# A hybrid decoder step on one core: the FFN's seven products in another order, and its two kinds of low parts on swapped engines

## The reference, cut to what matters

```
u = rmsnorm(x, g_ffn) @ w_up              # 1024 -> 4096
x = x + jnp.square(jax.nn.relu(u)) @ w_down   # 4096 -> 1024
y = rmsnorm(x, g_final)
```

## Time and profile before

| | us |
|---|---|
| median of three runs | 1503.9 |
| the profiled execution, its own time | 1504.5 |
| its span, first to last instruction | 1502.7 |
| PE busy in the span | 1412.1 (94%) |
| DVE busy | 1020.5 (68%) |
| POOL busy | 602.2 (40%) |
| ACT busy | 532.2 (35%) |

### The profile page before, as it was taken

One profiled execution on the slowest core, in us unless ns is written; L12 is line 12 of the kernel. 1 busy time (PEld: TensorE's weight loads), 2 busy tenths in 40 slices (PEclk: granted clock), 3 DMA queues, 4 the chain that ended last, 5 costly groups with the idle time before them and its releaser, 6 DMA issues.

```text
span 1502.7 us, 28686 instructions
## 1 busy us (share of the span) xinstructions
PE 1412.1 (94%) x11826; PEld 1242.5 (83%) x11826; DVE 1020.5 (68%) x1759; ACT 532.2 (35%) x917; POOL 602.2 (40%) x454
## 2 busy tenths in 40 slices
PE   6999999999999889898997999999999999999996
PEld 4989989999998566685777979797988989797984
DVE  6883655568852677664527895958687685958588
ACT  6342322322221567543313333332323333332324
POOL 2121221888710000002218572827456372827453
PEclk9999999999999999999999999999999999999998
DMA  7412103722206732297000322131303122131312
GB/s 210 169 42 61 29 15 62 111 67 75 63 8 216 278 120 71 101 384 258 29 3 29 114 67 104 56 114 41 108 23 128 43 87 84 56 115 43 114 32 116
DMA packets 109811, 144.59 MB, mean 96 GB/s; under 512 B 26738, under 2 KB 78774, under 8 KB 107762
## 3 DMA queue, kind: packets, MB, share of 16 engines
q1 hardware_dynamic: 107618, 138.04, 29.3%
q0 software_dynamic: 2064, 4.72, 0.8%
HBM read 126.31 MB, written 21.14 MB: 98 GB/s over the span
## 4 chain that ended last, share of the span: by engine, by line
PE 78%; DVE 11%; issue 6%; ACT 3%; POOL 1%; DMA 1%; SPq 0%; DVEq 0%; ACTq 0%; POOLq 0%
PE PS L343 7%; PE PS L344 7%; PE PS L345 7%; PE PS L2706 6%; PE PS L2708 6%; PE PS L2707 6%; PE PS L2745 5%; PE PS L2746 5%; PE PS L2747 5%; PE PS L1647 2%; PE PS L1668 2%; PE PS L1687 2%; PE PS L2199 2%; PE PS L2201 2%; PE PS L2200 2%
## 5 line engine op out<-in xcount | busy, mean ns | idle before, releaser
L2745 PE MATMUL PS<-R_wb,R_ua 128*128 128x512 f32 x448 | 178.0, 397 | 10.9 <-DVE R_ua L2951 8.8
L2973 DVE TENSOR_TENSOR R_x<-R_x,PS 128x512 f32<-128x512 f32 x256 | 161.5, 677 | 20.1 <-PE PS L2747 20.1
L2746 PE MATMUL PS<-R_wb,R_ua 128*128 128x512 f32 x448 | 174.7, 390 | 0.0
L2747 PE MATMUL PS<-R_wb,R_ua 128*128 128x512 f32 x448 | 174.6, 390 | 0.0
L2874 POOL TENSOR_TENSOR R_wb<-R_slot,R_wb 128x1024 fp32r<-128x1024 f32 x56 | 146.0, 2607 | 42.0 <-ACT R_wb L2782 42.0
L2623 DVE TENSOR_TENSOR R_wb<-R_slot,R_wb 128x1024 fp32r<-128x1024 f32 x56 | 83.2, 1486 | 98.0 <-ACT R_wb L2617 98.0
L604 POOL TENSOR_TENSOR R_w<-R_wstage,R_w 128x1024 fp32r<-128x1024 f32 x29 | 75.0, 2589 | 176.2 <-ACT R_w L599 176.2
L2782 ACT ACTIVATE R_wb<-R_slot 128x1024 fp32r<-128x1024 f32 x56 | 59.4, 1060 | 240.1 <-PE PS L2747 131.7
L343 PE MATMUL PS<-xn_high,R_w 128*128 128x352 f32 x384 | 125.9, 328 | 3.2 <-ACT R_hscr L733 2.0
L343 PE MATMUL PS<-R_w,xn_low 128*128 128x256 f32 x432 | 125.6, 291 | 0.0
L344 PE MATMUL PS<-xn_low,R_w 128*128 128x352 f32 x384 | 123.2, 321 | 2.2 <-issue 2.2
(11 more groups left out here) (441 smaller groups left out, 3848.3 us busy)
## 6 DMA issues: line engine op xcount, KB each, us to landing
R_slot<-in_w_up SPq DMA_DIRECT2D x32, 512.0 KB, 3.9
R_slot<-in_w_down SPq DMA_DIRECT2D x32, 512.0 KB, 3.3
R_t<-x_sums SPq DMA_DIRECT2D x7, 2112.0 KB, 7.7
R_wstage<-in_w_in SPq DMA_DIRECT2D x28, 512.0 KB, 4.2
R_cache<-in_cache_attn_v SPq DMA_DIRECT2D x56, 256.0 KB, 8.9
R_cache<-in_cache_attn_k SPq DMA_DIRECT2D x28, 256.0 KB, 5.8
R_cache<-in_cache_attn_k SPq DMA_DIRECT2D x7, 1024.0 KB, 9.7
bias_by_distance_copies<-bias_by_distance POOLq DMA_DIRECT2D x1, 4608.0 KB, 27.2
```

What stands on the lines that cost most here:

```text
L2745: pe.matmul(out, ul[:, f, ts], wh[:, f, :], start=(f == 0 and k in OPENS), stop=False, skip_group_check=True)
L2746: pe.matmul(out, uh[:, f, ts], wl[:, f, :], start=False, stop=False, skip_group_check=True)
L2747: mm = pe.matmul(out, uh[:, f, ts], wh[:, f, :], start=False, stop=(f == 1), skip_group_check=True)
L2973: ins = dve.tensor_tensor(part, part, PS[:, product_bank(k, p), :], ALU.add)
```

## The change

`STEPS` goes from P1 P2 P6 P7 P4 P5 P3 to P1 P2 P5 P6 P7 P4 P3. `up_low_part` goes from DVE to POOL and `right_low_part` from POOL to DVE. The sums are built in another way (S1 first, then S3, S2, S4; T1 first, then T2 and the rest), and the hidden sums of the down half are one on DVE (s1) and three on POOL, where two were on each. The sample tokens' product is issued inside the last hidden step, before its fourth unit. The slots of the weights follow the new order.

```diff
-        P1, P2, P6, P7, P4, P5, P3 = STEPS = range(7)
+        P1, P2, P5, P6, P7, P4, P3 = STEPS = range(7)
...
         def phase_f2_gps(pool):
+            up_low_part(pool, 0, P1)
             for q in (5, 6, 7):
...
-            up_low_part(dve, 0, P1)
             x_taken(dve, 7)
...
             def hidden_step(b, k):
...
+                    elif k == P5:
+                        pe.wait_ge(u_added, summed_count(b, P2, p))
...
+                    if k == P3 and p == 3:
+                        sample_product(b)
...
         def phase_g_act(act):
...
+                up_high_part(act, b, P4)
+                if not b:
+                    sum_high("t4", t4h, XS4, ALL)
                 for p in UNITS[P7]:
                     kept(b, P7, p)
-                up_high_part(act, b, P5)
+                up_high_part(act, b, P3)
                 left_high_part(b, P1)
-                up_high_part(act, b, P3)
                 right_high_part(b, P1)
...
         def phase_g_gps(pool):
             for b in range(NBLK):
+                quarter_in(pool, b, "a21")
+                quarter_in(pool, b, "a22")
+                if b:
+                    pool.wait_ge(right_split, 7 * b)
+                pool.tensor_tensor(sa, a21, a22, ALU.add).then_inc(pool_sums, 1)
+                up_low_part(pool, b, P2)
                 pool.wait_ge(up_split, 7 * b + P1 + 1)
                 pool.tensor_tensor(a11, a11, a21, ALU.subtract).then_inc(pool_sums, 1)
+                pool.wait_ge(pool_sums, sums_count(b, W_S3))
+                pool.tensor_tensor(a21, a22, a11, ALU.subtract).then_inc(pool_sums, 1)
+                up_low_part(pool, b, P5)
                 if not b:
+                    pool.wait_ge(norm_split, low_made("T2"))
+                    pool.tensor_tensor(XS4[:, :, LATE], x21[:, :, LATE], XS2[:, :, LATE], ALU.subtract).then_inc(f_split, 1)
+                    sum_low("t3 early", t3l, XS3, t3h, EARLY)
+                    sum_low("t3 late", t3l, XS3, t3h, LATE)
...
+                pool.tensor_tensor(a12, a12, a21, ALU.subtract).then_inc(pool_sums, 1)
+                up_low_part(pool, b, P6)
+                up_low_part(pool, b, P7)
                 if not b:
                     sum_low("t4 early", t4l, XS4, t4h, EARLY)
                     sum_low("t4 late", t4l, XS4, t4h, LATE)
+                up_low_part(pool, b, P4)
+                up_low_part(pool, b, P3)
                 pool.wait_ge(up_split, 7 * b + P3 + 1)
...
                 pool.tensor_tensor(w11, w22, ta, ALU.subtract).then_inc(pool_sums, 1)
+                pool.wait_ge(u_added, sum_count(b))
+                pool.tensor_tensor(q21, q11, q21, ALU.subtract).then_inc(pool_sums, 1)
+                pool.wait_ge(pool_sums, sums_count(b, H_S3))
+                pool.wait_ge(left_split, 7 * b + P1 + 1)
+                pool.tensor_tensor(q11, q22, q21, ALU.subtract).then_inc(pool_sums, 1)
                 pool.tensor_tensor(w12, w22, w12, ALU.subtract).then_inc(pool_sums, 1)
...
                 pool.tensor_tensor(w21, w21, w11, ALU.subtract).then_inc(pool_sums, 1)
...
+                pool.tensor_tensor(q12, q12, q11, ALU.subtract).then_inc(pool_sums, 1)
+                if b < NBLK - 1:
+                    up_low_part(pool, b + 1, P1)
...
         def phase_g_dve(dve):
...
+                for p in (0, 1):
+                    summed(b, P4, p)
                 left_low_part(b, P1)
+                right_low_part(b, P1)
+                for p in (2, 3):
...
+                right_low_part(b, P2)
...
+                dve.tensor_tensor(s1, q21, q22, ALU.add).then_inc(u_added, 1)
                 for p in range(4):
                     added(b, P1, p)
                 added(b, P2, 0)
+                right_low_part(b, P5)
+                left_low_part(b, P5)
+                for p in range(1, 4):
+                    added(b, P2, p)
+                added(b, P5, 0)
+                right_low_part(b, P6)
                 left_low_part(b, P6)
...
+                right_low_part(b, P3)
+                left_low_part(b, P3)
```

More of the change, by code:

```diff
@@ L2428, in x_taken @@
             j = F2_ORDER[q]
-            for kk in (range(2) if q < 4 else (1, 0)):
+            for kk in range(2):
                 dve.wait_ge(xs2_T, 2 * q + kk + 1)
@@ L2508, in program @@
                 SLOT_OF[b, name] = slot
-            for name, slot in zip(("w11", "w12", "w21", "w22", "ta"), (sa, a22, a11, a21, a12)):
+            for name, slot in zip(("w11", "w21", "w12", "w22", "ta"), (sa, a21, a11, a22, a12)):
                 SLOT_OF[b, name] = slot
-            order5 = tuple(SLOT_OF[b, name] for name in ("w11", "w12", "w21", "ta", "w22"))
+            order5 = tuple(SLOT_OF[b, name] for name in ("ta", "w11", "w12", "w21", "w22"))
         LOADS = [(b, name) for b in range(NBLK) for name in ("a11", "a12", "a21", "a22", "w11", "w21", "w12", "w22")]
@@ L2541, in program @@
         ND, NU = 1 + 7 * 4, 7 * 4
[L2542 to L2547, removed]
+        W_S1, W_S3, W_S2, W_S4, W_T1, W_T2, H_S3, H_S2, W_T3, W_T4, H_S4 = range(11)
+        HIGH_ORDER = [("up", k) for k in STEPS] + [("left", P1), ("right", P1), ("left", P2), ("right", P2)] + [
+            (side, k) for k in (P5, P6, P7, P4, P3) for side in ("right", "left")]
+        KEPT, KEPT_AS = (P1, P5, P6, P7), {P1: u11, P5: u22, P6: u12, P7: u21}
+        SUMMED, SUMMED_AS = (P2, P7, P4, P3), {P2: u11, P7: u22, P4: u21, P3: u12}
+        SQUARED = ("u11", "u22", "u21", "u12 early", "u12 late")
         u_psum, u_kept, u_added, u_squared = sem("u_psum"), sem("u_kept"), sem("u_added"), sem("u_squared")
@@ L2848, in phase_g_act @@
                     tile_squares(NCH)
-                for k in (P6, P7, P4, P5, P3):
+                for k in (P5, P6, P7, P4, P3):
                     right_high_part(b, k)
                     left_high_part(b, k)
-                    if last and k == P5:
-                        roots(0)
+                if last:
+                    roots(0)
                 if not last:
@@ L2870, in phase_g_gps @@
         def phase_g_gps(pool):
-            def right_low_part(b, k):
-                high, low = wb[(7 + k) % 2]
-                pool.wait_ge(operand_high, high_count(b, "right", k))
-                pool.tensor_tensor(low, slot(b, RIGHT[k]), high.bitcast(F32), ALU.subtract).then_inc(right_split, 1)
             def sum_low(what, low, part, high, c):
@@ L2946, in scaled, with right_low_part @@
                 dve.scalar_tensor_tensor(y, y, stat[:, 3, i:i + 1], gain, ALU.mult, ALU.mult).then_inc(xs2_ready, 1)
+            def right_low_part(b, k):
+                high, low = wb[(7 + k) % 2]
+                dve.wait_ge(operand_high, high_count(b, "right", k))
+                dve.tensor_tensor(low, slot(b, RIGHT[k]), high.bitcast(F32), ALU.subtract).then_inc(right_split, 1)
             def left_low_part(b, k):
@@ L3039, in phase_g_dve @@
                 added(b, P7, 0)
+                right_low_part(b, P4)
                 left_low_part(b, P4)
@@ L3052, in phase_g_dve @@
                     added(b, P4, p)
-                added(b, P5, 0)
-                left_low_part(b, P3)
-                for p in range(1, 4):
-                    added(b, P5, p)
                 if not last:
-                    up_low_part(dve, b + 1, P1)
                     for p in range(4):
```

232 lines of the change are left out of this document (97 added, 135 removed).

## The result

The changed kernel takes 1554.66 us (median of 6 runs, 1551.75 to 1559.1) beside 1503.51 of the kernel before on the same chip (6 runs): the ratio is 1.0344, with a 95% interval of 1.0327 to 1.036. It is slower by 3.4%; 1547 was forecast. Its profiled execution took 1554.5 with a span of 1552.7, so 50.0 of span have to be explained.

A forecast was written before the change was run, and what follows sets the result against it. PE was taken as the bound (82.0 of 84.1 us a block), so only its waits could change. 1504.5 + 28.8 (eight blocks) + 14 (block 0) = 1547.3, put at 1547; range for 8 in 10: 1522 to 1566.

The forecast's parts named there:

- The mechanism of the down half: Down steps: VectorE's low-part pairs and GpSimd's sums lock each other out, the waiting engine going next; +2.5 a block.
- The first rival: Down half: VectorE keeps the lock over both low parts of a pair; a block gains 2.2, total 1529 us; chance 0.18.
- The sample product: Before P3's fourth unit: PE waits 1.9 instead of 0.77 for VectorE's half square; +1.1 a block.
- The hidden half: Hidden steps of later blocks: GpSimd's low parts come in time, cost 0; 0.6 a block if DVE's square falls in.
- A later block: Blocks after the first: each goes from 84.1 to about 87.7; the sum counts eight at 3.6, 28.8.
- Block 0: First block: GpSimd's queue delays P6 to 837.5, P4 by 12, P3 to 864; own cost +14, bounds 0 and +17.
- The meetings in GpSimd's queue: First block, up to P6's low part: DVE's locking instructions come between GpSimd's own 23.0, adding 8.4.
- The clock rival: Every block: P5's wait of 2.7 brings half clock, 2.8 each time, total 1569 us; chance 0.11.
- the low parts ahead of P3: Down half's end: two low parts behind seven additions end at 37.6, PE done with P4 at 36.8: wait 0.8.
- the rival "no change": Down half's locks hardly meet: blocks gain 4 in all, the first block costs +4, total 1504 us; chance 0.05.

The follow-up runs named there:

- Experiment 1: Changed kernel with GpSimd's sums w12, w21 and q12 each made to wait until VectorE's pair of low parts for P5, P6 and P7 is done: 1525.48 us, ratio 1.0152.
- experiment 2: Changed kernel with P1's right low part on VectorE moved behind the half square that the sample product waits for: 1533.98 us, ratio 1.0213.
- Experiment 9: Changed kernel with the up weights' low parts back on VectorE from block 1 on, nothing else moved: 1543.65 us, ratio 1.0267.
- experiment 3: Changed kernel with GpSimd's queue reordered in block 0 alone and t4's high part made earlier on ScalarE: 1540.13 us, ratio 1.025.
- experiments 4 and 8: Changed kernel with the engines exchanged back and the step order kept: 1545.84 us; the same with three places in GpSimd's queue changed: 1536.14 us.
- three added up: Changed kernel with GpSimd's sums behind VectorE's pairs, the half square ahead of P1's right low part, and block 0's queue reordered: 1492.1 us, ratio 0.9928.
- two more: Kernel with three edits, plus sample product behind P3's fourth unit and, in block 0, P2's sums ahead of x's low part: 1496.91 us, ratio 0.9962.
- experiment 4: Changed kernel with right low parts back on GpSimd, up low parts on VectorE from block 1, step order kept: 1545.84 us, ratio 1.0288.

## Why the prediction was right, and where its sizes were off

**The mechanism of the down half** held in each of its steps. Counted from the first down step of block 2 (1049.58), P5's right low part was to end at 10.2 and ended at 9.9, the left one 13.55 and 13.25, P6's right one 19.3 and 18.9. Forecast waits: 2.7, 1.4 and 0.8; found: 2.26, 1.07 and 0.58. Each is shorter by 0.2 to 0.4, but a step behind a wait is itself 0.15 to 0.3 longer, so the down half lost 4.8 over seven steps of 5.44, where 4.9 was forecast. Experiment 1 shows the cause: with the three sums out of the pairs, 3.6 of it is gone.

**The first rival,** that VectorE's pair is not broken, is refuted by w12 at 1058.38 in block 2, and by the 29 us that experiment 1 brought back. The Trainium skill's rule of the exclusive lock (SBUF — State Buffer, section SBUF: two separate sides) agrees with every meeting shown here (w12, 2.40 long by itself, ends 2.24 behind the low part that it met). It does not decide between the forecast and this rival; that the waiting engine goes next is this case's finding.

**The sample product** waited 2.22 instead of 1.9: ta ended at 1041.59, 2.2 into P3's step (from 1039.43) and not 1.8, because it had itself come behind the left low part of P1. The chain was right (experiment 2 took away 1.9 of the 2.2), but the profile put the wait down to "issue", not to VectorE's square as forecast.

**The hidden half** was forecast at 0 in its steps, and all seven took 5.81 to 5.86. Experiment 9 shows that the low parts on GpSimd were not free for all that: 0.75 a block comes from P3's low part through ta. It lay in the forecast of the sample product's wait and was not seen as a price of that half of the change.

**A later block** was forecast at 87.7 and took 88.13. Over eight blocks that is 32.1 instead of 28.8.

**Block 0** cost 114.41 - 88.13 = 26.3 over a later block, where before it was 12.7: +13.5, forecast +14. P6 started at 835.68 (837.5), P4 11.75 behind P6's end (12), P3 at 863.79 (864). Two errors cancelled there. The meetings in GpSimd's queue cost 6.9 (835.68 less 805.83, sa's start, less the queue's own 23.0; 0.9 of it GpSimd stood idle) where 8.4 was counted, and the half clock lengthened two steps (P6's to 7.99, P4's to 8.37 instead of 5.85) where 2.8 was taken once. It came behind the waits ahead of P2 and P5 too (steps of 7.63 and 7.60 at a granted clock of 0.78), but both were followed by a wait that took up what they lost. And P5's wait of 3.1 was not for GpSimd's queue, as the prediction had it, but for VectorE's sum of P2; that is hidden in the same total, and became visible when experiment 3 put the queue right.

**The clock rival** was forecast not to come in later blocks, and it came in some: behind a wait of 2.2 the sample product ran at a granted clock of 0.66 in blocks 4 and 7, between the 1.2 and 2.4 GHz levels, which cost 1.63 each time (5.08 - 3.45). That is 3.3 that the sum did not have. In blocks 3 and 6 it came behind the wait of 2.2 ahead of P5: that down step ran at 0.75, but P6's wait of 1.1 was gone by it, so these blocks are only 0.1 to 0.2 longer. The last block's P4 step, which waits for the token sum as before and now ran at half clock behind it, added 1.8 (9.38 against 7.61).

Together: 32.1 + 13.5 + 3.3 + 1.8 = 50.7 against 50.0 of span; the forecast was 42.8. The mechanism was right; the sizes missed are the clock (5) and the sample product's wait (3).

**Two slips in the prediction's sums** change nothing in the forecast. By its own terms the low parts ahead of P3 end at 37.7, not 37.6. And the rival "no change" puts block 0's low end at +4, where the bound given before is 0; with 0 that rival stands at 1500, not 1504.

What stays open: whether the exchange of engines or the order of the steps costs more. With the engines back and the order kept (experiments 4 and 8) blocks stay at 86 to 88, and with the exchange kept and four instructions moved they are 82.7, so with the queues tried neither by itself sets the time. The old order with the engines exchanged was not run, and no arrangement of the new order with the down weights' low parts on GpSimd was found that has no sum ahead of a low part.

## What to carry to other kernels

When two engines share a lock, the length of an instruction in the profile is its own time plus what is left of the other engine's instruction that it meets, and two instructions back to back on one engine are not one critical section. Put work that nobody waits for (here three sums, taken up 10 us later or more) behind the pair that somebody waits for, by a semaphore wait, before moving work between the engines. Taking away one wait moves everything queued behind it, so run the edits together as well as one by one: here three added up, and two more took back 5 us.

## What was not expected of the hardware

The tensor engine's granted clock did not fall behind every wait of one length: of the seven sample products behind a wait of 2.2 in the changed kernel, two were at half clock; three of seven in experiment 1, one of seven behind 1.86 in experiment 4, none behind 1.5 in experiment 9. A wait of 2.2 thus cost 2.2 in some blocks and 3.9 in others.

A square with one tensor as both of its inputs is held up by GpSimd as two different ones are: 2.61 instead of 1.26 in experiment 2.
